# Seven-product feed-forward on one Trainium2 core: the third product accumulates in the first one's bank, and the fifth moves its high and low operands in one 512-column pass

## What is computed

```python
for i in range(2):                       # mixers: short convolution, then latent attention
    x = x + mixer_i(rms_norm(x, norm_mix_g[i]))
    h = rms_norm(x, norm_ffn_g[i])
    x = x + (silu(h @ w_gate[i]) * (h @ w_up[i])) @ w_down[i]
return rms_norm(x, final_norm_g)
```

## Time and profile before

| | |
|---|---|
| median of 3 runs | 1072.54 us (1072.46 to 1074.56) |
| the profiled execution, its own time | 1072.86 us |
| its span | 1071.0 us |
| TensorE's granted clock, mean of the span | 0.999 of full speed |
| busy: PE, PEld, DVE, ACT, POOL | 99%, 88%, 75%, 45%, 21% of the span |
| 256-column matmuls of the seven products | 3696 (3 lines of 1232) |

### The profile page before, as it was taken

One profiled execution on the slowest core, in us unless ns is written; L12 is line 12 of the kernel. 1 busy time (PEld: TensorE's weight loads), 2 busy tenths in 40 slices (PEclk: granted clock), 3 DMA queues, 4 the chain that ended last, 5 costly groups with the idle time before them and its releaser, 6 DMA issues.

```text
span 1071.0 us, 18469 instructions
## 1 busy us (share of the span) xinstructions
PE 1060.9 (99%) x6666; PEld 946.0 (88%) x6666; DVE 802.5 (75%) x1106; ACT 478.8 (45%) x715; POOL 224.4 (21%) x211
## 2 busy tenths in 40 slices
PE   8999999999999999999999999999999999999997
PEld 7888888999999998888888766789999999988897
DVE  5755659999999999544455678599999999975343
ACT  6312236644444446222346777465444444552222
POOL 6000001323323320122110355013232232102110
PEclk9999999999999999999999999999999999999999
DMA  7334242232332332432436511113323323342311
GB/s 200 105 91 117 78 118 79 80 118 81 115 117 81 115 108 79 138 94 85 120 99 146 136 53 40 41 40 118 109 88 117 109 87 117 110 111 81 116 59 79
DMA packets 144008, 106.54 MB, mean 99 GB/s; under 512 B 4488, under 2 KB 140096, under 8 KB 143968
## 3 DMA queue, kind: packets, MB, share of 16 engines
q1 hardware_dynamic: 143392, 104.80, 32.9%
q0 software_dynamic: 544, 1.21, 0.4%
q10 hardware_dynamic: 32, 0.01, 0.0%
HBM read 99.72 MB, written 2.10 MB: 95 GB/s over the span
## 4 chain that ended last, share of the span: by engine, by line
PE 96%; DVE 2%; DMA 1%; issue 0%; ACT 0%; POOL 0%; SPq 0%; DVEq 0%; ACTq 0%
PE ps L429 29%; PE ps L431 29%; PE ps L430 29%; PE ps L1735 3%; PE ps L1796 2%; PE ps L1812 2%; DMA x_nat<-in_x 1%; DVE op_w_lo L573 1%; PE ps L1778 0%; PE ps L1777 0%; PE ps L1779 0%; DVE w_sum L1140 0%; PE ps L488 0%; POOL prob L723 0%; PE ps L1869 0%
## 5 line engine op out<-in xcount | busy, mean ns | idle before, releaser
L429 PE MATMUL ps<-x_op_hi,op_w_hi 128*128 128x256 f32 x1232 | 349.2, 283 | 0.7 <-DVE op_w_lo L573 0.7
L430 PE MATMUL ps<-x_op_lo,op_w_hi 128*128 128x256 f32 x1232 | 348.6, 283 | 0.0
L431 PE MATMUL ps<-x_op_hi,op_w_lo 128*128 128x256 f32 x1232 | 348.6, 283 | 0.0
L429 PEld LDWEIGHTS ps<-x_op_hi,op_w_hi 128*128 128x128 f32 x1232 | 236.5, 192 | 2.4 <-issue 1.1
L430 PEld LDWEIGHTS ps<-x_op_lo,op_w_hi 128*128 128x128 f32 x1232 | 236.5, 192 | 0.1
L431 PEld LDWEIGHTS ps<-x_op_hi,op_w_lo 128*128 128x128 f32 x1232 | 236.5, 192 | 0.0
L413 DVE TENSOR_TENSOR wgt_lo<-raw,wgt_hi 128x1024 fp32r<-128x1024 f32 (+5 forms) x119 | 128.5, 1095 | 80.0 <-ACT wgt_hi L400 78.9
L429 PE MATMUL ps<-hid_hi,wgt_hi 128*128 128x512 f32 x476 | 186.7, 392 | 0.0
L431 PE MATMUL ps<-hid_hi,wgt_lo 128*128 128x512 f32 x476 | 185.3, 389 | 0.0
L430 PE MATMUL ps<-hid_lo,wgt_hi 128*128 128x512 f32 x476 | 185.3, 389 | 0.0
L400 ACT ACTIVATE wgt_hi<-raw 128x1024 fp32r<-128x1024 f32 (+5 forms) x119 | 99.4, 848 | 141.6 <-PE ps L431 134.6
(11 more groups left out here) (186 smaller groups left out, 1355.1 us busy)
## 6 DMA issues: line engine op xcount, KB each, us to landing
pair_raw<-in_ffn_w_gate SPq DMA_DIRECT2D x22, 1024.0 KB, 5.3
pair_raw<-in_ffn_w_up SPq DMA_DIRECT2D x22, 1024.0 KB, 5.3
raw<-in_conv_w_in SPq DMA_DIRECT2D x24, 512.0 KB, 3.7
raw<-in_ffn_w_down SPq DMA_DIRECT2D x28, 384.0 KB, 3.2
raw<-in_ffn_w_down SPq DMA_DIRECT2D x28, 320.0 KB, 2.9
raw<-in_conv_w_out SPq DMA_DIRECT2D x8, 512.0 KB, 3.5
raw<-in_mla_w_o SPq DMA_DIRECT2D x8, 512.0 KB, 4.6
raw<-in_ffn_w_down SPq DMA_DIRECT2D x5, 512.0 KB, 4.7
```

What stands on the lines that cost most here:

```text
L429: nc.tensor.matmul(acc, wh, xh, start=first, stop=False)
L430: nc.tensor.matmul(acc, wh, xl, start=False, stop=False)
L431: return nc.tensor.matmul(acc, wl, xh, start=False, stop=last)
```

## The change

The low data operands are laid behind the high ones in one array `x_op` (same bytes, same places). Product 2 no longer starts a sum of its own in bank 1: it goes on adding in bank 0, onto product 0, once ACT has copied product 0 out as s1. The bank then holds u2, which ACT copies out (`copy_u2`); `u2` has one place in all groups. Product 4 has bank 1 for itself: one matmul of 512 columns puts high weights by high data in one half and high weights by low data in the other, and a second one of 256 columns adds low weights by high data to the first half. DVE adds s1 and the halves in two instructions of 256 columns, one ahead of part 1 and one behind it.

```diff
-        x_op_hi, _, e = place("x_op_hi", [P, DC // 2, OPS, N], F32R, XG_END - 8 * DC // 2 * OPS * N)
-        x_op_lo, _, e = place("x_op_lo", [P, DC // 2, OPS, N], F32R, e)
+        x_op, _, e = place("x_op", [P, 2, DC // 2, OPS, N], F32R, XG_END - 8 * DC // 2 * OPS * N)
+        x_op_hi, x_op_lo = x_op[:, 0], x_op[:, 1]
...
+                def copy_u2(g, op0, bank):
+
+                    wait(sc, op_used, op0 + 3)
+                    wait(sc, w_u3_done, g)
+                    nc.scalar.activation(u2, ps[:, bank, 0:N], ACT.Copy).then_inc(u2_done, 1)
+
                 def group(i, par, first=False):
...
                     wait(sc, op_used, op0 + 1)
-                    wait(sc, u2_done, g)
+                    wait(sc, s1_read, g)
                     nc.scalar.activation(s1[:, :], ps[:, 4 * par, 0:N], ACT.Copy).then_inc(s1_done, 1)
                     make_op_hi(sc, *nxt, 0)
                     if first and par == 0:
                         norm_rows(sc, n_root)
+                    copy_u2(g, op0, 4 * par)
                     if par:
                         wait(sc, gate_new, i + (PAIRS_F * l + 1))
...
                     hidden_hi(0)
+                    copy_u2(g, op0, 4)
                     sc.wait_ge(gate_new, PAIRS_F * l + i + 1)
...
-                    halves = ps[:, b0 + 1, :].rearrange("p (h n) -> p h n", h=2)
-                    twice = s1[:, :].unsqueeze(1).broadcast_to([P, 2, N])
-                    if par and last:
-                        u_2 = u2
-                        nc.vector.tensor_tensor(pair[:, 3, :], halves[:, 0, :], s1[:, :], ALU.add)
-                        nc.vector.tensor_tensor(u2, halves[:, 1, :], s1[:, :], ALU.add).then_inc(u2_done, 1)
-                    elif par:
-                        u_2 = quarters[:, ds(i * 4 + 4, 1), :].rearrange("p a n -> p (a n)")
-                        nc.vector.tensor_tensor(quarters[:, ds(i * 4 + 3, 2), :], halves, twice, ALU.add).then_inc(u2_done, 1)
-                    else:
-                        u_2 = u2
+                    if not par:
                         wait(ve, h_new, i + PAIRS_F * l)
-                        nc.vector.tensor_tensor(gate_u2[:, 3:5, :], halves, twice, ALU.add).then_inc(u2_done, 1)
+                    nc.vector.tensor_tensor(to[:, 3, :], ps[:, b0 + 1, 0:N], s1[:, :], ALU.add).then_inc(s1_read, 1)
                     weights(1)
+                    wait(ve, s1_read, g + 1)
+                    nc.vector.tensor_tensor(to[:, 3, :], ps[:, b0 + 1, N:S], to[:, 3, :], ALU.add).then_inc(c11_done, 1)
                     wait(ve, u2_done, g + 1)
                     nc.vector.tensor_tensor(w_u3[:, :, :], ps[:, b0 + 2, :].rearrange("p (h n) -> p h n", h=2),
-                                            u_2.unsqueeze(1).broadcast_to([P, 2, N]), ALU.add).then_inc(w_u3_done, 1)
+                                            u2.unsqueeze(1).broadcast_to([P, 2, N]), ALU.add).then_inc(w_u3_done, 1)
...
-                bank, half = ((0, 0), (2, 0), (1, 1), (2, 1), (1, 0), (3, 1), (3, 0))[p]
+                bank, half = ((0, 0), (2, 0), (0, 0), (2, 1), (1, 0), (3, 1), (3, 0))[p]
...
+                    if p == 2:
+                        wait(pe, s1_done, g + 1)
...
+                    begins, ends = k == 0 and p != 2, k == DC // 2 - 1
+                    if p == 4:
+                        both = ps[:, 4 * par + bank, :].rearrange("p (h n) -> p h n", h=2)
+                        nc.tensor.matmul(both, op_w_hi[:, p, col], x_op[:, :, k, x, :], start=begins, stop=False)
+                        ins = nc.tensor.matmul(acc, op_w_lo[:, p, col], x_op_hi[:, k, x, :], start=False, stop=ends)
+                    else:
+                        ins = product(acc, op_w_hi[:, p, col], op_w_lo[:, p, col],
+                                      x_op_hi[:, k, x, :], x_op_lo[:, k, x, :], begins, ends, p == 2)
```

More of the change, by code:

```diff
@@ L260, in trunk_kernel @@
         sum_done, sum_ve, op_hi, op_lo, op_used = sem("sum_done"), sem("sum_ve"), sem("op_hi"), sem("op_lo"), sem("op_used")
-        s1_done, u2_done, w_u3_done, c12_done = sem("s1_done"), sem("u2_done"), sem("w_u3_done"), sem("c12_done")
+        s1_done, s1_read, w_u3_done, c12_done = sem("s1_done"), sem("s1_read"), sem("w_u3_done"), sem("c12_done")
+        c11_done, u2_done = sem("c11_done"), sem("u2_done")
         set_read, gate_new, act_done, res_new = sem("set_read"), sem("gate_new"), sem("act_done"), sem("res_new")
@@ L425, in prepare, with product @@
             make(eng, name, i + ahead // ub, ahead % ub)
-        def product(acc, wh, wl, xh, xl, first, last):
-            nc.tensor.matmul(acc, wh, xh, start=first, stop=False)
-            nc.tensor.matmul(acc, wh, xl, start=False, stop=False)
-            return nc.tensor.matmul(acc, wl, xh, start=False, stop=last)
+        def product(acc, wh, wl, xh, xl, first, last, onto=False):
+            nc.tensor.matmul(acc, wh, xh, start=first, stop=False, skip_group_check=onto)
+            nc.tensor.matmul(acc, wh, xl, start=False, stop=False, skip_group_check=onto)
+            return nc.tensor.matmul(acc, wl, xh, start=False, stop=last, skip_group_check=onto)
         def tile_wait(eng, name, i, t):
@@ L858, in last_group @@
                     sc.wait_ge(op_used, op0 + 1)
-                    sc.wait_ge(u2_done, g)
+                    sc.wait_ge(s1_read, g)
                     nc.scalar.activation(s1[:, :], ps[:, 4, 0:N], ACT.Copy).then_inc(s1_done, 1)
@@ L877, in last_group @@
                         hidden_hi(q)
-                    sc.wait_ge(u2_done, g + 1)
+                    sc.wait_ge(c11_done, g + 1)
                     unit_hi(sc, name, 0, 3)
@@ L1275, in group @@
                     wait(ve, w_u3_done, g + 1)
+                    wait(ve, c11_done, g + 1)
                     nc.vector.tensor_tensor(to[:, 2, :], ps[:, b0 + 3, N:S], w_u3[:, 0, :], ALU.add).then_inc(c12_done, 1)
@@ L1648, in seven_product @@
                     col = slice(k * P, (k + 1) * P)
-                    ins = product(acc, op_w_hi[:, p, col], op_w_lo[:, p, col],
-                                  x_op_hi[:, k, x, :], x_op_lo[:, k, x, :], k == 0, k == DC // 2 - 1)
+                    begins, ends = k == 0 and p != 2, k == DC // 2 - 1
[6 more added lines that the diff above has]
+                                      x_op_hi[:, k, x, :], x_op_lo[:, k, x, :], begins, ends, p == 2)
                 if ks[-1] == DC // 2 - 1:
```

## The result

The changed kernel takes 1076.99 us (median of 6 runs, 1076.42 to 1079.07) against 1072.70 us of the kernel before (1072.43 to 1074.56, on the same chips). The ratio is 1.0046, 95% interval [1.0036, 1.0055]: slower by 4.3 us, where 2.3 had been forecast. A second set of runs gave 1.0049 [1.0035, 1.0063]. One execution in all that follows (of the kernel with moved code, 1305.4 us at a mean granted clock of 0.752) fell into a slow state and is left out. The profiled execution had 1078.34 us and a span of 1076.5.

What follows compares the result with a forecast made beforehand. PE bounds the kernel (96% of the span), with DVE's chain close beside it. DVE's late start, less its spare, plus PE's restart moves the layers by 1.24 and 1.04, together 2.3 us: 1074.8 us, range 1072.2 to 1079.

Steps and rivals of the forecast that it cites:

- the likeliest case: Late start in group 0 carried by DVE to each layer's third down unit: 1074.8 us, interval 1073.5 to 1076, chance 0.62.
- a stretched loop: Added add partly unhidden in DVE's loop, 0.05 to 0.1 us a group, setting the range's upper end, 1079.
- The wait of product 2 in group 0: PE waits for ACT's copy of s1 at each layer's phase start: 2.24 us plus about 0.1 for restart.
- The chain from the late statistic to DVE's part 1: Group 1: late statistic and added u2 copy delay ACT's part 1, and so DVE's, by 1.29 us, never won back.
- The third down unit as the place where it is paid: End of each layer's phase: PE newly waits about 0.6 us there for DVE's late low weights.
- Product 4: Merged matmul on PE saves 0.0133 us a step, 0.053 a group, 2.35 for the kernel, on PE's chain alone.
- The added add at nothing: DVE's second add behind part 1, at most 0.41 us, hides under POOL's hold on part 2; costed at nothing.
- the rival with 1088: Added add unhidden on DVE in every group: 0.34 us a group, 13.6 in all beside the 2.3; chance 0.1.
- The clock: After PE's idles the clock falls to 1.2 GHz; 3 us of it in both layers costs 3 us, 1078; chance 0.03.

Runs made afterwards that it cites:

- kernel with moved code: Changed kernel with the first copy of s1 made early, plus eight always-met DVE waits before its second feed-forward phase: 1074.73 us, ratio 1.002.
- changed (2): Profiled execution of the changed kernel's second set, nothing altered, clock not falling; the set measured 1077.76 us, ratio 1.0049.
- product 4 in three: Changed kernel with product 4 back to three matmuls of 256 columns a step and without the second DVE add: 1076.6 us, ratio 1.0038.
- the unit first: Changed kernel with the third down unit's low weights made before hidden 3 to 5 in the last group: 1076.61 us, ratio 1.0038.

## Why the prediction was right and wrong

The range of 1072.2 to 1079.0 held the result. The mechanism of the likeliest case is the one that came, but its own interval, 1073.5 to 1076, was missed: 4.3 us came where it had 2.3. That the range held it is in part luck, since its upper end had been put there for a stretched loop, and what filled it were three things that the sum did not have. At full clock ("changed (2)") the two phases are 3.65 us longer. The forecast's own terms, the late start of DVE less what DVE had been ahead of PE at the unit, and the 0.05 us from its weights to PE's start, give 2.05 of it (1.13 and 0.92, forecast 1.24 and 1.04). The unhidden add at the ends gives 0.66, the loops 0.93: 1.17 more in layer 1, by the late issues, and 0.24 less in layer 0, where the kernel before had late DMAs and this one had none. The fall of the clock in some executions comes on top. By its steps:

- **The wait of product 2 in group 0: right in both layers.** 2.34 us were forecast with the restart, 2.28 came, and the wait alone, put into the kernel before, showed it.
- **The chain from the late statistic to DVE's part 1: right.** 1.29 forecast, 1.21 to 1.23 measured at full clock. DVE did not win it back by its own pace, as forecast. Layer 0 as a whole: 1.24 forecast, 1.05 and 1.23 measured. How near these are is luck: at the last part 1 DVE was only 0.81 and 0.99 us late, since the late DMAs were before's alone, and the unhidden add put 0.33 on it again.
- **The third down unit as the place where it is paid: right, its sizes not.** A wait of 0.6 us was forecast; it was 0.1 to 0.3 in layer 0 and 1.0 in layer 1. In layer 0 it was short because PE itself came later than forecast, 0.93 and 0.95 us at the down projection's first matmul instead of 0.67: the saving was 0.59 smaller, and the waits that it got back were 0.7 to 0.8 and not 0.5. In layer 1 the late issues made it long. With the weights made earlier it was gone, and 1.0 us with it.
- **Product 4: mis-sized by half.** A merged step was to save 0.0133 us and saved 0.0066, a group 0.027 and not 0.053. The price was taken from a run of like matmuls of 512 columns; here a wide and a narrow one alternate, and the pair takes 0.353 us where the two paces add up to 0.347. The term did not decide the end of a phase, since DVE set it, in layer 0 by a little. All of it is worth 0.6 us where DVE lets it show.
- **The added add at nothing: right in the loop, wrong at its ends.** The loop stayed at 10.03 us, and the rival with 1088 fell. But the last gate group has no cover, and there it cost 0.33 us a layer. Put alone into the kernel before, where it comes once more in the last group, and in an execution with a late DMA, such an add cost 1.35 us in all. "It costs nothing" had been shown for a steady group and then used for 22.
- **Not in the sum: the late issues of DVE in layer 1, 1.2 us.** That an instruction of a loop is issued 0.1 us later by the place of its code was no term and no rival. They show because DVE's loop had no spare.
- **The clock: a chance of 0.03 was too low.** It was given from a stretch in which PE was half busy and the clock stayed up. Five kernels or sets had the wait at the phase's start (the changed one twice, the wait alone, product 4 in three, the unit first). In three of their five profiled executions the clock fell, each time at one of the two starts and at a price of 1.5 us, and by their times it did in about half of all (15 of 27 lie 0.5 us or more above the rest of their kernel); in none of the others' profiles did it fall there. The median has its share. The rival's form was right (the 1.2 GHz level for some 3 us); it had put the fall into both layers of each execution, for 3 us in all.

The Trainium skill ("TensorE: Matmul & The Clock Gate", section "Back-to-back issue gap") had given one saved instruction 2.5 ns, the rows before 13.3. The trace of the changed kernel lies between them, 6.6 ns. The section says beside its formula that it is for an isolated matmul, and that in a stream of weight loads and matmuls both together set the pace.

What stays open: why the clock falls in one execution and not in the next, after the same wait; and what it is at that place in DVE's stream that delays the issue. That it goes away with the instructions moved was shown in one pair of kernels, and no more than that.

## What to carry to other kernels

Where two engines run side by side with a few hundredths of spare, cost the first and last rounds by themselves: there the cover of the steady state is missing, and what is late at the start is late at the end. A wait put at a phase's start must be followed through the engine that copies for it, since what it had still to do first is the length of the wait; to give that copy an earlier place took the whole wait away. And before a slow loop is put down to its work, move its code by a few instructions and look whether it stays.

## What the hardware showed beyond the forecast

- The same instruction of DVE in a loop started 45 ns after the end of its wait, or, in every second group, 142 to 151 (the first time 396), and moving the loop's code by four instructions took that away.
- After a wait of 2.12 us of a PE that had been busy until then, the granted clock fell to 0.50 for 3.4 us in some executions (in the others it stayed at 1.00). The fall came 0.38, 0.07 and 0.02 us after PE had started again, and matmuls of 256 columns then started 0.213 us apart instead of 0.120.
- A matmul of 512 columns and one of 256 in turn took 0.353 us a pair, each with its weight load; of one kind only it is 0.2267 and 0.120.
